# Sharing a third channel group of a depthwise convolution between three engines, and taking the key transposes out of the sample group's fixed order, in a hybrid decoder layer

## The chip, the cores and the metric

The kernel runs on one core of one Trainium2 chip. The metric is the time of one launch of the program on the device, in microseconds (us), and less is better. In the text PE is TensorE, DVE is VectorE, ACT is ScalarE, POOL is GpSimd and SP is the engine that issues most transfers.

## The reference

One layer of a decoder is computed for 512 prompt tokens and for 64 sample tokens (8 sequences of 8). Cut to what the change touches:

```python
a_glu, b_glu, q, k, v, qi, ki, wi, g_c, g_a = jnp.split(h @ w_in, IN_SPLITS, axis=-1)
glu = a_glu * jax.nn.sigmoid(b_glu)
buf = jnp.concatenate([conv_prefix, glu], axis=1)
# 31 taps per channel, 512 channels = 4 groups of 128 partitions
c = silu(layer_norm(causal_depthwise_conv(buf, conv_w, conv_b), lnc_g, lnc_b))
conv_branch = c @ w_conv_out
# sample tokens: indexer scores over 4096 cached keys, the best 256, then attention over them
idx, valid = select_keys(indexer_scores(qi, wi, ki_all), q_pos, topk)
kg = jnp.where(sel, cache_k[layer, phys, off], gather_rows(k_new, nidx))
vg = jnp.where(sel, cache_v[layer, phys, off], gather_rows(v_new, nidx))
o = attend_selected(q, kg, vg, valid)
mix = (sigmoid(g_c) * conv_branch + sigmoid(g_a) * (o @ w_attn_out)) @ w_o
```

After that come a layer norm, a mixture of 32 experts, a gated side branch and a second layer norm, which the change leaves alone. Everything is float32.

## The kernel before, in words

All work of the layer stands in one list of jobs, `JOBS`. Every engine walks through the same list and does its share of each job; semaphores count what is ready. The list has these stages.

**First stage (to about 86 us).** Keys of the indexer are fetched and turned, and the scores of the 64 sample tokens are made.

**Second stage (to about 346 us).** DVE picks the best 256 keys, eight at a time, in 32 rounds (L1962 to L1964). While it does, PE runs the input projections and ten gate jobs, each job one PSUM bank of four that take turns (`RING = 4`): a job may start only when ACT has emptied the bank of the job four places earlier. ACT empties every job and, right after some of them, makes "products" for the convolution: one tap times the gated input, 816 columns (`conv_product`, L1629; the first of a channel group is L1622). Which product stands after which job is written out in `PRODUCTS`, worked out from the jobs' costs. POOL adds the products up (`conv`, L1048), with three product buffers between the two engines: ACT may be three products ahead and then waits. Two channel groups of the four (`PCONV = 2`) are done in this way. The gated input of a channel group is POOL's too (`gated`, L1014 to L1018), and it needs that group's `aS` job. Between the adds stand four pieces of the page lookup (`physical_rows`, L1027 to L1034): each turns the page numbers of one chunk of the selected keys into cache rows, and waits until DVE has finished the chunk. `MAP_AT` says before which add the second and third stand. When the fourth is done, DVE merges the two lists of each token, PE turns the list (`offs`, L1295), ACT writes the offsets, and POOL can begin to gather.

**Third stage (about 346 to 745 us).** The 64 sample tokens are worked in 16 groups of four. For each group POOL issues eight gathers of keys and eight of values (L1069, two per token and kind). For groups 0 to 7 the keys are turned on PE (`T`, L1179, four jobs per group, each two banks of four transposes) and copied by ACT (L1645). For groups 8 to 15 DVE makes the logits itself (`KQ`, L2037 and L2042). Then come the logits (`QK`: L1191 and L1209), a maximum on DVE (L2167), the exponentials on ACT (L1651), the turned weights (`PT`, L1218 and L1219), the values (`PV`, L1227 and L1230), a mask on DVE (L2179) and a sum over groups (`OS`, L1237). There is one set of buffers for keys and one for values: POOL gathers the keys of group g+1 once the logits of group g are done, and the values of group g+1 once the values of group g have been used. POOL's order is keys, values, keys, values.

Beside it run the prompt's attention (`pi`, `qk`, `pt`, `pv` on PE; rounds, `unit` and `weigh` on DVE), the rest of the convolution branch (`cv`, `cn`, `cbP`, `cbS`) and the gates (`gaP`, `gaS`). The other two channel groups of the convolution, 62 taps, are DVE's there (`conv_tap`, L2052 and L2054, two instructions per tap); `cv` cannot start before they are done.

The order of this third stage comes from `merged`: it takes the next job from one of three streams (sample, prompt, branch) as the letters of `PICKS` say, and lays out DVE's work by its own costs, with taps and rounds as filling. In the sample stream the order within a group is fixed: QK, EX, PT, the first two T of the next group, PV, the last two T, OS.

**The rest (745 to 1268 us).** Output projections, layer norm, router, experts, second layer norm.

## Time and profile before

| | |
|---|---|
| runs of the kernel before, us | 1278.06, 1266.98, 1277.57 |
| median | 1277.57 |
| the profiled execution | 1269.41, its span 1267.6 |
| PE busy | 1138.5 (90%) |
| DVE busy | 744.5 (59%) |
| ACT busy | 432.1 (34%) |
| POOL busy | 537.0 (42%) |
| PE busy in the third stage (345 to 745 us) | 336.1 of 400 |
| gathers of keys and values | 256 issues, 264.4 us busy |

The span is the time from the first to the last instruction of one execution; the rest of the launch lies around it. Shares of busy time are averages over stages with different limits, so the rows that count are those of one stage: which engine has no gaps there, and what the last of the engines waits for. In the second stage DVE has none, in the third stage several engines take turns.

### The profile page before, as it was taken

How to read it: one execution, taken by the hardware profiler on the slowest of the kernel's cores; microseconds unless marked ns; L12 is line 12 of the kernel's file. 1: busy time of each engine (PE TensorE's matmuls, PEld its weight loads, DVE VectorE, ACT ScalarE, POOL GpSimd, SP SyncE). 2: the span in 40 equal slices, each digit the busy share in tenths (PEclk: the TensorE clock that was granted, in tenths of full speed). 3: DMA queues.
4: the chain of work that ended last, by engine and by line, in shares of the span. 5: the costliest groups of instructions: out<-in, count | busy, mean ns of one | idle time of the engine just before them, and what ended most of it. 6: DMA issues, size and time to landing. Idle time of an engine off the chain costs nothing.

```text
span 1267.6 us, 22339 instructions
## 1 busy us (share of the span) xinstructions
PE 1138.5 (90%) x8697; PEld 725.2 (57%) x8697; DVE 744.5 (59%) x1368; ACT 432.1 (34%) x952; POOL 537.0 (42%) x488
## 2 busy tenths in 40 slices
PE   4899999989989767668999999999999999999896
PEld 4525677778654333324556645888885555555442
DVE  1459999999998888787764513444533221111116
ACT  4540124364354366666322212123112222222220
POOL 5000067887876765576677700000003433433310
PEclk9899999989999887778999999999899999998998
DMA  9511222223166565586799853024278999999935
GB/s 323 214 47 42 85 75 70 67 75 104 50 198 172 169 200 166 150 252 202 226 315 299 284 179 105 17 73 161 84 275 323 403 418 411 369 419 415 417 116 194
DMA packets 86200, 258.61 MB, mean 204 GB/s; under 512 B 13311, under 2 KB 45939, under 8 KB 77191
## 3 DMA queue, kind: packets, MB, share of 16 engines
q1 hardware_dynamic: 54816, 168.79, 35.7%
q0 software_dynamic: 28720, 84.98, 21.1%
q10 hardware_dynamic: 2559, 3.40, 0.8%
q8 instruction: 70, 1.15, 0.4%
q14 instruction: 35, 0.29, 0.1%
HBM read 356.78 MB, written 19.05 MB: 296 GB/s over the span
## 4 chain that ended last, share of the span: by engine, by line
PE 45%; DVE 29%; DMA 13%; POOL 7%; issue 4%; ACT 1%; SPq 1%; DVEq 0%; POOLq 0%; ACTq 0%
DMA arena<-in_w_ex 9%; POOL arena L1069 7%; PE ps L1522 7%; DVE arena L1963 6%; DVE arena L1962 6%; DVE arena L1964 6%; PE ps L1139 6%; PE ps L1145 5%; PE ps L1369 4%; PE ps L1544 3%; PE ps L1361 3%; DMA arena<-in_w_in 2%; PE ps L1532 2%; DMA arena<-in_cache_kv,arena 2%; PE ps L1227 2%
## 5 line engine op out<-in xcount | busy, mean ns | idle before, releaser
L1069 POOL DMA_INDIRECT arena<-in_cache_kv,arena x256 | 264.4, 1033 | 118.5 <-issue 73.7
L1139 PE MATMUL ps<-arena 128*128 128x288 f32 (+2 forms) x1120 | 294.4, 424 | 1.1 <-ACT arena L1688 1.1
L1139 PEld LDWEIGHTS ps<-arena 128*128 128x128 f32 (+1 forms) x1120 | 209.6, 189 | 83.3 <-issue 30.3
L1522 PE MATMUL ps<-arena 128*32 128x256 f32 x2144 | 145.4, 388 | 17.1 <-DMA arena<-in_w_ex 16.1
L1095 POOL DMA_INDIRECT scr_ypair<-arena x67 | 66.9, 999 | 165.7 <-ACT arena L1896 161.2
L2359 DVE TENSOR_TENSOR arena<-arena,ps 128x64 f32<-128x64 f32 x67 | 14.9, 222 | 183.3 <-ACT arena L1890 183.3
L1611 ACT ACTIVATE arena<-ps 128x256 f32<-128x256 f32 (+5 forms) x138 | 57.6, 428 | 183.1 <-PE ps L1361 57.2
L1048 POOL TENSOR_TENSOR arena<-arena 128x816 f32<-128x816 f32 x58 | 103.0, 1775 | 17.4 <-ACT arena L1629 10.6
L1145 PE MATMUL ps<-arena 128*128 128x256 f32 (+4 forms) x544 | 105.3, 357 | 0.8 <-ACT arena L1833 0.6
L1145 PEld LDWEIGHTS ps<-arena 128*128 128x128 f32 (+1 forms) x544 | 92.4, 194 | 13.3 <-issue 1.8
L1522 PEld LDWEIGHTS ps<-arena 128*32 128x32 f32 x2144 | 66.3, 111 | 56.8 <-issue 21.9
L1089 POOL DMA_INDIRECT arena<-scr_x,arena x34 | 35.4, 1040 | 145.9 <-DVE arena L2338 135.3
L1962 DVE MAX8 arena<-arena 128x8 f32<-128x2052 f32 x32 | 73.6, 2299 | 1.1
L1544 PE MATMUL ps<-arena 128*32 128x256 f32 x1072 | 72.6, 388 | 1.0 <-issue 0.9
L1963 DVE FIND_INDEX8 arena<-arena 128x8 uint32<-128x2052 f32 x32 | 73.3, 2290 | 0.0
L1964 DVE MATCH_REPLACE8 arena<-arena 128x2052 f32<-128x2052 f32 x32 | 73.0, 2280 | 0.0
L1179 PE MATMUL ps<-arena 128*128 128x128 f32 x256 | 42.5, 320 | 33.6 <-DMA arena<-in_cache_kv,arena 25.7
L1629 ACT ACTIVATE arena<-arena 128x816 f32<-128x816 f32 x60 | 57.0, 970 | 28.6 <-POOL arena L1048 26.3
L1361 PE MATMUL ps<-arena 128*128 128x288 f32 (+1 forms) x192 | 64.1, 483 | 0.0
L1179 PEld LDWEIGHTS ps<-arena 128*128 128x128 f32 x256 | 34.1, 165 | 47.6 <-DMA arena<-in_cache_kv,arena 31.8
L2054 DVE SCALAR_TENSOR_TENSOR arena<-arena 128x512 f32<-128x512 f32 x120 | 56.9, 516 | 2.0
L2037 DVE TENSOR_TENSOR arena<-arena 128x1024 f32<-128x1024 f32 x32 | 39.2, 1224 | 30.4 <-DMA arena<-in_cache_kv,arena 29.4
(342 smaller groups left out, 1649.2 us busy)
## 6 DMA issues: line engine op xcount, KB each, us to landing
arena<-in_w_ex SPq DMA_DIRECT2D x67, 2048.0 KB
arena<-in_w_ex SPq DMA_DIRECT2D x67, 1024.0 KB
arena<-in_w_in SPq DMA_DIRECT2D x20, 1024.0 KB, 5.6
arena<-scr_q SPq DMA_DIRECT2D x32, 256.0 KB, 5.0
arena<-in_cache_kv,arena POOLq DMA_INDIRECT x256, 3.9
arena<-in_w_o SPq DMA_DIRECT2D x4, 1024.0 KB, 5.3
arena<-in_w_pg SPq DMA_DIRECT2D x4, 1024.0 KB, 6.1
arena<-scr_ypair SPq DMA_DIRECT2D x4, 1024.0 KB, 7.9
```

The lines of the kernel that those rows point to most:

```text
L1048: nc.gpsimd.tensor_tensor(a[:, 0:CLEN], a[:, 0:CLEN], p[:, 0:CLEN], ALU.add).then_inc(conv_add, 1)
L1069: pl.indirect_dma_start(unit_rows[:, 2 * j + t, half * H * HD:(half + 1) * H * HD], None, I["cache_kv"].rearrange("n (h d) -> (n h) d", h= ...
L1095: pl.indirect_dma_start(S["ypair"].rearrange("n (h d) -> (n h) d", h=4), bass.IndirectOffsetOnAxis(ap=slist[:, q:q + 1], axis=0), ys[q % Y ...
L1139: mm = nc.tensor.matmul(out, w[:, k], hT[:, k, a:b], start=(k == 0), stop=(k == KC - 1))
L1145: mm = nc.tensor.matmul(out, hT[:, k, at:at + rows], w[:, k], start=(k == 0), stop=(k == KC - 1))
L1179: mm = nc.tensor.transpose(PS[4 + m % 2][:, c * P:(c + 1) * P], unit_rows[:, 2 * j + t, c * P:(c + 1) * P], ident)
L1361: mm = nc.tensor.matmul(ps[:, 0:n], w[:, c], src[:, c, at:at + n], start=(c == 0), stop=(c == CC - 1))
L1522: mm = nc.tensor.matmul(PS[2 + q % 2][r:r + BLK, 0:F], xT[:, p % 3, j, 64 * h + BLK * sub:64 * h + BLK * sub + BLK], w[:, 4 * h + j, half, ...
L1544: mm = nc.tensor.matmul(PS[5 + q % 2][BLK * quarter:BLK * quarter + BLK, 0:D // 4], hidT[:, q % 2, c, :], w[:, c, quarter * (D // 4):(quar ...
L1962: step(V.max(m, work))
L1963: V.max_index(idxu[:, r * 8:r * 8 + 8], m, work)
L1964: step(V.match_replace(work, m, work, TAKEN))
```

## The change

Of the third channel group 12 taps are taken from DVE. ACT makes twelve more products for them, and POOL adds them up (11 adds) and writes the partial sum to where DVE then goes on from tap 12. So POOL makes 71 adds in place of 60 and DVE 50 taps in place of 62. The projection jobs are ordered so that each `aS` job comes after its own `bP`, `bS`, `aP` (b and a alternate for each channel group of 128), the products start after the fifth of these jobs and not after the ninth, and the pieces of POOL's other work get new places: the first page lookup before add 8, the second before add 34, the third before add 60, and the gated inputs of the second and third channel groups before adds 20 and 48. `AWAY` holds three stretches of the products' calendar in which none is planned.

The jobs that turn keys (or multiply them) become a stream of their own, `key_jobs`, with a letter `k` in `PICKS`; only two rules bind it: no key job of group g before the logits of group g-1, and no logits before the four key jobs of their group. The planner's time from a gather's issue to its landing goes to 3.5, and `PICKS` is new.

The diff, with the old letters of `PICKS` cut:

```diff
+SHARED = 12
+TAPS = [CW] * PCONV + [SHARED, 0]
+ADDS = sum(n - 1 for n in TAPS if n)
...
 def sample_jobs():
-    def keys(g):
-        return [("KQ" if g >= BY_VECTOR else "T", g, j) for j in range(GQ)] if g < NGR else []
-    jobs = keys(0)
     for g in range(NGR):
-        turned = keys(g + 1)
-        jobs += [("QK", g), ("EX", g), ("PT", g)] + turned[:2] + [("PV", g)] + turned[2:] + [("OS", g)]
+        jobs += [("QK", g), ("EX", g), ("PT", g), ("PV", g), ("OS", g)]
     return jobs
+def key_jobs():
+    return [("KQ" if g >= BY_VECTOR else "T", g, j) for g in range(NGR) for j in range(GQ)]
...
-    waiting = [("conv", c, w) for c in range(PCONV, CC) for w in range(CW)]
+    waiting = [("conv", c, w) for c in range(PCONV, CC) for w in range(TAPS[c], CW)]
...
-            landed[("T", g, j) if keys else ("PV", g)] = pool + (2.3 if keys else 2.8)
+            landed[("T", g, j) if keys else ("PV", g)] = pool + LANDING
...
+        if job[0] in ("T", "KQ") and job[1]:
+            return ("QK", job[1] - 1) not in pe_end
+        if job[0] == "QK":
+            return ("KQ" if job[1] >= BY_VECTOR else "T", job[1], GQ - 1) not in jobs
...
-HOP, GATHER, TABLE = 0.12, 2.62, 1.28
+HOP, GATHER, LANDING, TABLE = 0.12, 2.62, 3.5, 1.28
+PICKS = ("pbpbpkkkpkppppspsbspppskppkpkksspspbsppppskkpkpkpsssbbskskkkpsppspspsbppskpkkpkbsppspspbsbksbkkkbpss"
...
     for g in range(2):
-        for kind in "ba":
-            for c in range(2):
+        for c in range(2):
+            for kind in "ba":
                 jobs += [(kind + "P", g, c), (kind + "S", g, c)]
...
-MAP_AT = {1: 21, 2: 46}
+MAP_AT = {0: 8, 1: 34, 2: 60}
+GATED_AT = {1: 20, 2: 48}
+AWAY = ((16.0, 27.0), (79.0, 90.0), (143.0, 152.0))
-_beside = RINGED[NUM[("bP", 1, 0)]:NUM[GATES[3][0]]]
-_pace = sum(cost(_j) for _j in _beside) / (PCONV * CW + 0.5)
+_beside = RINGED[NUM[("bP", 0, 1)]:NUM[GATES[3][0]]]
+def beside_pool(t):
+    return t - sum(min(max(t - a, 0.0), b - a) for a, b in AWAY)
+_pace = beside_pool(sum(cost(_j) for _j in _beside)) / (sum(TAPS) + 0.5)
 for _j in _beside:
-    _due += cost(_j) / _pace
-    _take = min(int(_due), PCONV * CW - _n)
-    PRODUCTS[_j] = range(_n, _n + _take)
+    _at += cost(_j)
+    _upto = min(int(beside_pool(_at) / _pace), sum(TAPS))
+    PRODUCTS[_j] = range(_n, _upto)
...
             def conv(c):
-                for w in range(1, CW):
+                for w in range(1, TAPS[c]):
                     for i, at in MAP_AT.items():
                         if k == at:
                             physical_rows(i)
+                    for i, at in GATED_AT.items():
+                        if k == at:
+                            gated(i)
...
-            for c in range(PCONV):
-                gated(c)
-            physical_rows(0)
-            for c in range(PCONV):
+            gated(0)
+            for c in range(PCONV + 1):
                 conv(c)
             physical_rows(3)
-            for c in range(PCONV, CC):
-                gated(c)
+            gated(PCONV + 1)
...
             def conv_tap(c, w):
-                if w == 0:
+                if w == TAPS[c]:
                     dve.wait_ge(glu_ready, 1 + 3 * c + 3)
+                if w and w == TAPS[c]:
+                    dve.wait_ge(conv_ready, c + 1)
+                    dve.wait_ge(conv_add, ADDS)
```

**Three places in the order of instructions.** First ACT, at the first products. The program names are few, since nearly all tiles lie in one tensor, `arena`, and the PSUM banks are `ps`; so the lines and shapes tell the instructions apart. Before, from the emptying of the ninth projection job (L1730) on; L1622 and L1629 are products, the others empty a job:

```order
L1730 ACTIVATE arena<-ps 128x288
L1622 ACTIVATE arena<-arena 128x816
L1739 ACTIVATE arena<-ps 128x288
L1629 ACTIVATE arena<-arena 128x816 x2
L1730 ACTIVATE arena<-ps 128x288
L1629 ACTIVATE arena<-arena 128x816
L1739 ACTIVATE arena<-ps 128x288
L1629 ACTIVATE arena<-arena 128x816 x2
```

In the change, from the emptying of the seventh to the twelfth job (the emptyings are L1745, L1753 with L1754, L1747 and L1756; L1646 is a product):

```order
L1745 ACTIVATE arena<-ps 128x288
L1646 ACTIVATE arena<-arena 128x816 x2
L1753 ACTIVATE arena<-ps 128x224
L1754 ACTIVATE arena<-ps 128x8x8
L1646 ACTIVATE arena<-arena 128x816 x2
L1747 ACTIVATE arena<-ps 128x288
L1756 ACTIVATE arena<-ps 128x288
L1745 ACTIVATE arena<-ps 128x288
L1753 ACTIVATE arena<-ps 128x224
L1754 ACTIVATE arena<-ps 128x8x8
L1646 ACTIVATE arena<-arena 128x816 x2
```

Products 4 to 7 stand after the seventh and eighth job, then come three jobs with none, and products 8 and 9 stand after the twelfth. Before, the first product came only after the ninth.

Second POOL, from its first gated input. Before (L1014 to L1018 a gated input, L1027 to L1034 the page lookup, L1048 an add):

```order
L1014 TENSOR_TENSOR arena<-arena 128x64
L1016 TENSOR_TENSOR arena<-arena 128x512
L1018 COPY arena<-arena 128x8x8
L1014 TENSOR_TENSOR arena<-arena 128x64
L1016 TENSOR_TENSOR arena<-arena 128x512
L1018 COPY arena<-arena 128x8x8
L1027 TENSOR_TENSOR arena<-arena 128x2560
L1031 TENSOR_TENSOR arena<-arena 128x1280
L1031 TENSOR_TENSOR arena<-arena 128x640
L1031 TENSOR_TENSOR arena<-arena 128x320
L1031 TENSOR_TENSOR arena<-arena 128x160
L1034 TENSOR_TENSOR arena<-arena 128x80
L1048 TENSOR_TENSOR arena<-arena 128x816 x21
```

In the change (L1031 to L1035 a gated input, L1044 to L1051 the page lookup, L1068 an add):

```order
L1031 TENSOR_TENSOR arena<-arena 128x64
L1033 TENSOR_TENSOR arena<-arena 128x512
L1035 COPY arena<-arena 128x8x8
L1068 TENSOR_TENSOR arena<-arena 128x816 x8
L1044 TENSOR_TENSOR arena<-arena 128x2560
L1048 TENSOR_TENSOR arena<-arena 128x1280
L1048 TENSOR_TENSOR arena<-arena 128x640
L1048 TENSOR_TENSOR arena<-arena 128x320
L1048 TENSOR_TENSOR arena<-arena 128x160
L1051 TENSOR_TENSOR arena<-arena 128x80
L1068 TENSOR_TENSOR arena<-arena 128x816 x12
```

The second gated input has gone from here to before add 20, and eight adds now stand ahead of the page lookup. The eighth of them needs product 8.

Third PE, sample group 2 from its turned weights to its sum over groups. Before (L1218 and L1219 PT, L1179 T of the next group, L1227 and L1230 PV, L1237 OS):

```order
L1218 MATMUL ps<-arena 128x128 x2
L1219 MATMUL ps<-arena 64x128
L1179 MATMUL ps<-arena 128x128 x16
L1227 MATMUL ps<-arena 8x512 x8
L1230 MATMUL ps<-arena 8x512 x4
L1179 MATMUL ps<-arena 128x128 x16
L1237 MATMUL ps<-arena 64x512
```

In the change (L1235 and L1236 PT, L1196 T, L1244 and L1247 PV, L1316 a score of the prompt, L1254 OS):

```order
L1235 MATMUL ps<-arena 128x128 x2
L1236 MATMUL ps<-arena 64x128
L1196 MATMUL ps<-arena 128x128 x8
L1244 MATMUL ps<-arena 8x512 x8
L1247 MATMUL ps<-arena 8x512 x4
L1196 MATMUL ps<-arena 128x128 x24
L1316 MATMUL ps<-arena 128x512
L1254 MATMUL ps<-arena 64x512
```

Of the four key jobs of the next group, two stood ahead of the values, and now one does; three stand behind.

## Rows read from the trace of the kernel before

**Rows 1.** Timeline of PE: start, length, line, wait in brackets; four starts of logits.

```profile
365.60 0.73 PE L1191 MATMUL ps<-arena 128*8 128x320 f32 x8
...
436.52 0.72 PE L1191 MATMUL ps<-arena 128*8 128x320 f32 x8
...
570.18 1.16 PE L1191 MATMUL ps<-arena 128*8 128x320 f32 x8
...
727.09 0.73 PE L1191 MATMUL ps<-arena 128*8 128x320 f32 x8
```

**Rows 2.** Busy time by window: window, length, PE, PEld, DVE, ACT, POOL, clock, DMA.

```profile
437.00:463.00 26.00, 19.69 (x143) 11.81 (x139) 22.45 (x77) 13.58 (x31) 17.14 (x18) 0.87 0.64 190
463.00:488.00 25.00, 18.18 (x133) 9.55 (x129) 21.41 (x73) 17.55 (x44) 15.25 (x17) 0.80 0.58 167
488.00:510.50 22.50, 15.19 (x127) 8.50 (x119) 21.15 (x61) 15.93 (x35) 15.33 (x17) 0.85 0.65 187
510.50:541.00 30.50, 20.65 (x153) 10.75 (x149) 24.04 (x68) 19.30 (x46) 16.87 (x19) 0.78 0.54 153
541.00:571.00 30.00, 19.55 (x131) 7.41 (x123) 23.46 (x61) 17.79 (x45) 22.41 (x22) 0.77 0.82 257
...
683.00:706.00 23.00, 23.00 (x173) 14.80 (x169) 11.38 (x14) 7.17 (x12) 17.20 (x18) 1.00 0.90 296
```

**Rows 3.** Instruction groups of GpSimd, 345 to 430 and 436 to 556 us.

```profile
L1069 POOL DMA_INDIRECT arena<-in_cache_kv,arena x56 | 62.5, 1116 | 22.9 <-issue 16.1 <-PE ps L1230 4.5 <-ACT arena L1772 2.2
...
L1069 POOL DMA_INDIRECT arena<-in_cache_kv,arena x79 | 76.8, 972 | 44.2 <-issue 22.5 <-PE ps L1230 21.7
```

**Rows 4.** Timeline of GpSimd at the fifth sample group.

```profile
453.57 0.95 POOL L1069 DMA_INDIRECT arena<-in_cache_kv,arena  x1 [0.30 <-issue]
458.50 0.94 POOL L1069 DMA_INDIRECT arena<-in_cache_kv,arena  x1 [3.98 <-PE ps L1230]
```

**Rows 5.** Timeline of PE, fourth and fifth sample groups.

```profile
424.90 1.97 PE L1179 MATMUL ps<-arena 128*128 128x128 f32 x8 [7.44 <-DMA arena<-in_cache_kv,arena]
...
455.32 1.90 PE L1227 MATMUL ps<-arena 128*8 128x512 f32 x16
```

**Rows 6.** Instruction groups of VectorE by shape, 340 to 785 us.

```profile
L2054 DVE SCALAR_TENSOR_TENSOR arena<-arena 128x512 f32<-128x512 f32 x60 | 45.1, 752 | 2.0
...
L2054 DVE SCALAR_TENSOR_TENSOR arena<-arena 128x64 f32<-128x64 f32 x60 | 16.8, 280 | 0.0
...
L2078 DVE MAX8 arena<-arena 128x8 f32<-128x256 f32 x16 | 6.8, 425 | 0.4
```

**Rows 7.** Timeline of GpSimd, 170 to 341 us.

```profile
170.69 0.31 POOL L1014 TENSOR_TENSOR arena<-arena 128x64 f32<-128x64 f32 x1 [6.03 <-ACT arena L1737]
...
172.49 4.46 POOL L1027 TENSOR_TENSOR arena<-arena 128x2560 f32<-128x2560 f32 x1
...
183.53 15.49 POOL L1048 TENSOR_TENSOR arena<-arena 128x816 f32<-128x816 f32 x8
...
299.35 3.61 POOL L1027 TENSOR_TENSOR arena<-arena 128x2048 f32<-128x2048 f32 x1 [2.46 <-DVE arena L1974]
...
308.44 24.37 POOL L1048 TENSOR_TENSOR arena<-arena 128x816 f32<-128x816 f32 x13
...
340.80 0.32 POOL L1034 TENSOR_TENSOR arena<-arena 128x32 f32<-128x32 f32 x1
```

**Rows 8.** Timeline of ScalarE, 158 to 186 us, then its products, 139 to 345 us.

```profile
158.50 0.41 ACT L1728 ACTIVATE arena<-ps 128x288 f32<-128x288 f32 x1 [3.47 <-PE ps L1139]
...
185.66 0.41 ACT L1739 ACTIVATE arena<-ps 128x288 f32<-128x288 f32 x1 [2.61 <-PE ps L1139]
...
L1629 ACT ACTIVATE arena<-arena 128x816 f32<-128x816 f32 x60 | 57.0, 970 | 28.6 <-POOL arena L1048 26.3 <-POOL arena L1051 2.1
```

**Rows 9.** Timelines of VectorE and PE, where the lists end.

```profile
341.95 1.20 DVE L1989 SCALAR_TENSOR_TENSOR arena<-arena 128x256 f32<-128x256 f32 x1
...
345.92 0.44 PE L1295 MATMUL ps<-arena 64*128 64x64 f32 x2 [2.90 <-DVE arena L1993]
```

More of the change, by code:

```diff
@@ L163, in sample_jobs @@
 def sample_jobs():
-    def keys(g):
-        return [("KQ" if g >= BY_VECTOR else "T", g, j) for j in range(GQ)] if g < NGR else []
-    jobs = keys(0)
+    jobs = []
     for g in range(NGR):
-        turned = keys(g + 1)
-        jobs += [("QK", g), ("EX", g), ("PT", g)] + turned[:2] + [("PV", g)] + turned[2:] + [("OS", g)]
-    return jobs
+        jobs += [("QK", g), ("EX", g), ("PT", g), ("PV", g), ("OS", g)]
+    return jobs
+def key_jobs():
+    return [("KQ" if g >= BY_VECTOR else "T", g, j) for g in range(NGR) for j in range(GQ)]
 def columns(kind):
@@ L191, in merged @@
 def merged(picks):
-    streams = {"sample": sample_jobs(), "prompt": prompt_jobs(), "branch": branch_jobs()}
+    streams = {"sample": sample_jobs(), "prompt": prompt_jobs(), "branch": branch_jobs(), "keys": key_jobs()}
     jobs, vector_order, ring, slots = [], [], [], []
@@ L360, in merged @@
     return dve, jobs, vector_order + waiting
-HOP, GATHER, TABLE = 0.12, 2.62, 1.28
-PICKS = ("pbpbpssppssppsspppbpppsppsppsppsspsbssspbspsssssppsssppsssssssssbsbppssbpssspsppsbpsbsppsbpsssbppssp"
-         "ssbpsbbsssppssbsspspspbppsssssppbppspsppspssspbsbppspppspppssppsppsspppppsspssbsppsppbpspppssbpsppsp"
-         "bppsbspbsssbsbssssbbsbsbbssbsbssssbsbsbssbsbsssbsssbssbpsssbsbssbsssbsssbssbsbsssbsbsbs")
-STREAM = {"s": "sample", "p": "prompt", "b": "branch"}
+HOP, GATHER, LANDING, TABLE = 0.12, 2.62, 3.5, 1.28
+PICKS = ("pbpbpkkkpkppppspsbspppskppkpkksspspbsppppskkpkpkpsssbbskskkkpsppspspsbppskpkkpkbsppspspbsbksbkkkbpss"
+         "spppsbkpskkbksppsppbspsppbkbpskkksppsppspbsppkppksppkkbbpspsppppspkkppskbspppbkpspppsppkpsppbkspspps"
+         "pkbpkpbbsskpbkkbsbspkbbsbsksbkbsbksbbkbsssbkskkbsbskbsksbksbsbkkbsskskbsbksbkbsssbsbsbs")
+STREAM = {"s": "sample", "p": "prompt", "b": "branch", "k": "keys"}
 ATTENTION, VJOBS = merged([STREAM[k] for k in PICKS])[1:]
@@ L482 @@
 CHUNKS = [(0, 80), (80, 160), (160, 224), (224, TOPS)]
-MAP_AT = {1: 21, 2: 46}
+MAP_AT = {0: 8, 1: 34, 2: 60}
+GATED_AT = {1: 20, 2: 48}
+AWAY = ((16.0, 27.0), (79.0, 90.0), (143.0, 152.0))
 CLEN = PRE + NP + NB * (PRE + NQ) - PRE
 PRODUCTS = {}
-_beside = RINGED[NUM[("bP", 1, 0)]:NUM[GATES[3][0]]]
-_pace = sum(cost(_j) for _j in _beside) / (PCONV * CW + 0.5)
-_n, _due = 0, 0.0
-for _j in _beside:
-    _due += cost(_j) / _pace
-    _take = min(int(_due), PCONV * CW - _n)
-    PRODUCTS[_j] = range(_n, _n + _take)
-    _n += _take
-    _due -= _take
-assert _n == PCONV * CW
+_beside = RINGED[NUM[("bP", 0, 1)]:NUM[GATES[3][0]]]
+def beside_pool(t):
+    return t - sum(min(max(t - a, 0.0), b - a) for a, b in AWAY)
+_pace = beside_pool(sum(cost(_j) for _j in _beside)) / (sum(TAPS) + 0.5)
+_n, _at = 0, 0.0
+for _j in _beside:
+    _at += cost(_j)
+    _upto = min(int(beside_pool(_at) / _pace), sum(TAPS))
+    PRODUCTS[_j] = range(_n, _upto)
+    _n = _upto
+assert _n == sum(TAPS)
 GROUP_AT = {g[2]: n for n, g in enumerate(WGROUPS)}
@@ L1046, in conv @@
                         pl.wait_ge(conv_add, k)
-                    if w < CW - 1:
+                    if w < TAPS[c] - 1:
                         nc.gpsimd.tensor_tensor(a[:, 0:CLEN], a[:, 0:CLEN], p[:, 0:CLEN], ALU.add).then_inc(conv_add, 1)
@@ L1053, in conv @@
                         nc.gpsimd.tensor_tensor(convo[:, c, 0:NP], a[:, 0:NP], p[:, 0:NP], ALU.add).then_inc(conv_add, 1)
[L1054 to L1057 removed]
+            gated(0)
+            for c in range(PCONV + 1):
                 conv(c)
             physical_rows(3)
[L1060 to L1063 removed]
+            gated(PCONV + 1)
+            pl.wait_ge(conv_ready, PCONV + 1)
+            pl.wait_ge(conv_add, ADDS)
             pl.wait_ge(drained, after("offs"))
@@ L1325, in _ @@
                     if a[0] == 0:
-                        pe.wait_ge(conv_ready, PCONV)
-                        pe.wait_ge(conv_add, PCONV * (CW - 1))
-                        pe.wait_ge(conv_dve, 2 * CW * (CC - PCONV))
+                        pe.wait_ge(conv_ready, PCONV + 1)
+                        pe.wait_ge(conv_add, ADDS)
+                        pe.wait_ge(conv_dve, 2 * (CW * (CC - PCONV) - SHARED))
                     for c in range(CC):
@@ L2055, in conv_tap @@
                     ins.then_inc(conv_dve, 1)
-                dve.wait_ge(conv_dve, 2 * ((c - PCONV) * CW + w) + 2)
+                dve.wait_ge(conv_dve, 2 * ((c - PCONV) * CW + w - SHARED) + 2)
             def head_score(t, h):
@@ L2060, in head_score @@
                 if (t, h) == (1, 0):
-                    dve.wait_ge(conv_ready, PCONV)
-                    dve.wait_ge(conv_add, PCONV * (CW - 1))
+                    dve.wait_ge(conv_ready, PCONV + 1)
+                    dve.wait_ge(conv_add, ADDS)
                 wi = kw[:, t, 64 + h:65 + h]
```

2 lines of the change are left out of this document (removed).

## The prediction

> **What bounds the kernel now.** I read three views, in this order. The table of busy time by window says which engine has no gaps. From 87 to about 345 us that is DVE with its rounds of top-k; PE and POOL only have to be ready when the lists are. From 345 to 745 us it changes. In the five sample groups from 437 to 571 us [rows 2] no engine is full: DVE is busy 112.5 of 134 us, PE 93.3, and TensorE's granted clock is 0.77 to 0.87. From 683 to 706 us PE is busy all 23.0. The timeline of PE then gives the cadence: from the logits of group 0 to those of group 3 it takes 70.9 us, to those of group 8 another 133.7, to those of group 15 another 156.9 [rows 1]. The waits say who sets it. POOL waits 21.7 us between 436 and 556 us for PE to have used the values, and 4.5 before 430 us [rows 3]. The timelines show how: the last key gather of group 4 starts at 453.57, and then POOL stands 3.98 us [rows 4], because the values of group 3 (PE at 455.32 [rows 5]) come in PE's order behind two key jobs of group 4, and those wait for keys that were issued only a few us before. It is a loop: keys late, values late, the next values' gathers late.
>
> Two things decide, then: when the lists are ready, and the cadence of groups 3 to 7. The part after 745 us hangs on the end of this stage and moves with it.
>
> **Part 1: twelve taps to ACT and POOL, second stage.** DVE saves 12 taps of 0.75 + 0.28 us [rows 6], 12.4 us, in the third stage. ACT makes 12 products more beside idle time. The question is whether POOL is still at its fourth page lookup when DVE has the last chunk, at about 335.5 us. I follow POOL. Jobs of PE come every (185.66 - 158.50) / 7 = 3.88 us [rows 8]. The gated input of the first channel group can start two jobs sooner. But product 8, which the eighth add needs, stands behind the twelfth job, which ACT empties at 185.66 [rows 8]; the first page lookup stands behind that add in POOL's order. With the two parts of the emptying and a product of 0.97 us [rows 8], add 8 can start at 187.2. The seven adds before it are done by about 175, so POOL stands idle for some 12 us, in the stretch that `AWAY` keeps free of products. From there it has no gap: add 8 until 189.1; lookups of 11.0 (172.49 to 183.53), 11.0 and 9.1 us (299.35 to 308.44), two gated inputs of 1.8 (170.69 to 172.49), and 63 adds, each 24.37 / 13 = 1.87 to 15.49 / 8 = 1.94 us [rows 7], less 1.2 us since the last add of each group is shorter. That ends at 189.1 + 31.1 + 3.6 + 116.6 to 121.0 = 340.4 to 344.8. The fourth lookup took 5.6 us (335.5 to 341.1 [rows 7]) and would now end at 346.0 to 350.4, not 341.1. DVE came to the place that needs it only at 341.95 [rows 9], 0.85 us later. So the lists, and with them all gathers, are 4.0 to 8.4 us late; I take 6.5. PE waited 2.90 us for the lists [rows 9]. It will itself be held up, since ACT, with three product buffers, waits for POOL before it empties banks. Four banks cover 3 x 3.88 = 11.6 us of that, less beside the short jobs that turn the prompt's keys; about 10 us of PE's idle fit under 2.9 + 6.5 + what the chain from list to offsets takes. I cost it at nothing, and this cover is the thinnest in the sum. The gated input of one channel group, 1.8 us, is no longer behind the fourth lookup, but it lay beside DVE's merging.
>
> **Part 2: the key stream, third stage.** In groups 0 to 2 PE has the same key, value and logit jobs as before; one gate job of about 4 us comes into these groups, and PE's wait of 7.44 us for keys [rows 5] goes. PE is then full. I take 1 us longer, bounds 3 shorter and 5 longer. In groups 3 to 7 the values now stand ahead of the key jobs or behind one of them, so that POOL's wait shrinks from about 4 us per group to about 1. What comes next as a limit? POOL's own issuing: 80 gathers x (0.972 + 0.30) us [rows 3] = 101.8. PE: 93.3 busy, less at a higher clock. DVE: 112.5 before; four taps (4.1), five of the smallest rounds (two instructions of about 0.43 each, 4.3 [rows 6]) and two prompt units leave this stretch, one large round comes, so about 104.5. DVE is the next limit, and it cannot be filled wholly: once per group it waits for the values, which wait for their gathers. I add 8.5 us of such waits, where 21.5 were before, and take 113, against 133.7: 20.7 saved. Bounds: 106 (27.7 saved), if the waits almost vanish, and 126 (8 saved), if DVE's place in the order makes the exponentials late as often as before. In groups 8 to 15 PE is full already; I take 1.5 us saved, bounds 5 saved and 2 lost. The twelve taps bring nothing on top: they are what lets DVE follow the new cadence.
>
> Of TensorE's clock: the five windows miss 0.13 to 0.23 of full speed, together 25 us of their 134 [rows 2], and the transposes that came after the wait of 7.44 us took 1.97 us [rows 5]. I count none of it, as DVE and POOL limit the new cadence. The Trainium skill, in TensorE: Matmul & The Clock Gate (HAM oscillation), says that an engine which waits for data again and again is put back to half its clock each time, and that the cost is half of the throttled time. By that rule PE itself would get up to 25 us back in these windows once it no longer waits, 4 us more than I count for them, and the sum would go to 1255 in place of 1259 (with the 4 us explained below). The trace agrees on the clock; whether that time is on the path it doesn't show.
>
> **The sum**, against the profiled execution of 1269.4 us (span 1267.6): + 6.5 + 1 - 20.7 - 1.5 = -14.7, so 1254.7. The median of the runs, 1277.6, is 8.2 above the profiled execution, since two of the three runs lie near 1278 and one at 1267. Nothing tells me where the median of the changed kernel falls between the two, and I take half of the difference: **1259 us**. All times below have the same 4 us in them.
>
> **The cases.**
>
> 1. As above: lists 4 to 8 us late, cadence 16 to 26 us better. 1259, by its bounds 1250 to 1270. For it: both steps can be counted out in rows. Chance 0.50.
> 2. POOL catches up, and the lists are not late: the idle 12 us are made up somewhere I do not see. 1259 - 6.5 = 1252. Against it: POOL's sum of work from 189 us has no gap left. Chance 0.10.
> 3. The cadence hardly moves, because DVE or ACT takes POOL's place: only 6 us are saved of the 21, the lists are late. 1259 + 15 = 1274. For it: DVE is busy 84% in these groups already [rows 2], and its order puts rounds ahead of maxima. Chance 0.24.
> 4. Slower. ACT stands at products that wait for POOL during the three lookups and the 12 us gap, PE's four banks run out, and the gate jobs end long after the lists. PE could lose as much as 11.0 + 11.0 + 9.1 us of lookups, 31 us, against an end of PE's work at 345.92 - 2.90 = 343.0 us [rows 9]; offsets would be made at 374 in place of 346, gathers 28 us late. With the cadence's 21 us that gives 1259 + 21.5 = 1280; it decides from the point at which PE stands for more than about 11 us before the lists. Against it: before, ACT's waits for POOL never stopped PE but for a few us. Chance 0.08.
> 5. More than forecast: with fewer waits PE is at its full clock, exponentials and copies come sooner, and groups 3 to 7 come near POOL's 102 us. 1259 - 11 = 1248. Chance 0.08.
>
> One that does nothing is not among them: the order of the instructions shows both moves.
>
> **Range and chances.** The range is 1243 to 1277: it takes in cases 1, 2, 3 and 5, with 4 us to either side for where the median falls. About 1% is what a measurement of this kernel can tell from no change. Against the median of 1277.6 the bound for faster is 1264.8: 0.40 of case 1, nearly all of 2 and 5, some 0.54 together. Slower by over 1%, above 1290, needs case 4 with a cadence like case 3's: 0.06. The rest, 0.40, is no change.
>
> **What would show it.** In the profile of the changed kernel: POOL idle from about 175 to 187 us, waiting for ACT; the first lookup from about 189 to 200; POOL's last add of the third channel group at 340 to 345; the first gather of keys at 352 to 356 in place of 347.7; PE waiting in the second stage for ACT, in all near 10 us; then logits of group 3 to logits of group 8 in 113 us (106 to 126), POOL's waits for PE at L1086 in all below 20 us, granted clock above 0.85, DVE busy over 90% in those groups; and the end of the third stage at 730 us. The forecast is wrong if the first gather does not move, if the cadence stays above 25 us a group, or if PE stands for more than 11 us before the lists.

## The result and the profile after

The changed kernel takes 1266.2 us (median of 20 runs, 1257.0 to 1271.2). The kernel before takes 1276.7 in the same comparison. The ratio is 0.991, with an interval of 0.990 to 0.993: 11 us faster. I had forecast 1259 us, 18.6 below the shown median. The direction and the range held; the gain was a little more than half of the forecast one. By the bound that I had set for faster, 1264.8 us, the result falls to what I had called no change (0.40), though the interval leaves out 1. One of the 20 runs of the kernel before took 1915.9 us; without it its median is 1276.6. The profiled execution took 1268.0 us, its span is 1266.3.

**First a common mark.** Two profiled executions differ before the change begins. The row of the first top-k instruction shows it (count; shortest, median, longest ns; start of the first and last). First the kernel before:

```profile
L1962 DVE MAX8 arena<-arena x32: 2299/2299/2301, 87.4 to 324.0; 128x8 f32<-128x2052 f32 x32
```

and the changed kernel:

```profile
L1979 DVE MAX8 arena<-arena x32: 2298/2299/2300, 92.8 to 328.7; 128x8 f32<-128x2052 f32 x32
```

The first stage has the same instructions in both and ended 5.4 us later here. So I count from the first MAX8, and end at the logits of group 15. That stretch was 727.1 - 87.4 = 639.7 us before and is 720.85 - 92.8 = 628.1 now: 11.6 us shorter, and the medians say 11.

**The cadence.** The timeline of PE of the changed kernel at logits 0, 3, 8 and 15, answering to [rows 1]:

```profile
384.91 1.25 PE L1208 MATMUL ps<-arena 128*8 128x320 f32 x8
...
451.60 0.72 PE L1208 MATMUL ps<-arena 128*8 128x320 f32 x8
...
561.86 1.26 PE L1208 MATMUL ps<-arena 128*8 128x320 f32 x8
...
720.85 0.73 PE L1208 MATMUL ps<-arena 128*8 128x320 f32 x8
```

The three pieces are 66.7, 110.3 and 159.0 us, where 70.9, 133.7 and 156.9 stood. The windows of the changed kernel (columns as in [rows 2]), groups 0 to 2, 3 to 7 and 8 to 14:

```profile
385.00:452.00 67.00, 62.64 (x415) 33.16 (x418) 58.77 (x130) 34.95 (x64) 51.11 (x48) 0.99 0.68 193
452.00:562.00 110.00, 84.99 (x631) 40.90 (x623) 100.10 (x304) 76.69 (x189) 78.60 (x81) 0.85 0.70 206
562.00:721.00 159.00, 149.51 (x1121) 91.21 (x1117) 104.05 (x180) 59.38 (x130) 116.58 (x114) 0.98 0.83 269
```

In groups 3 to 7 DVE is now busy 100.1 of 110 us, 91%. POOL's waits in the third stage (line waited at, who is waited for, sum, times, longest), first the one for the values in the kernel before, then those of the changed kernel:

```profile
POOL arena L1069 <- PE ps L1230: 42.5, 13, 8.4
...
POOL arena L1086 <- PE ps L1247: 17.4, 10, 4.8
POOL arena L1086 <- ACT arena L1789: 2.9, 1, 2.9
POOL arena L1086 <- PE ps L1226: 2.2, 2, 1.9
```

POOL stood 42.5 us for the values, and now it stands 17.4.

**The lists.** POOL's timeline of the changed kernel around the first and the fourth page lookup:

```profile
176.98 3.97 POOL L1068 TENSOR_TENSOR arena<-arena 128x816 f32<-128x816 f32 x2 [0.24 <-ACT arena L1646]
192.50 1.63 POOL L1068 TENSOR_TENSOR arena<-arena 128x816 f32<-128x816 f32 x1 [11.55 <-ACT arena L1646]
194.09 4.46 POOL L1044 TENSOR_TENSOR arena<-arena 128x2560 f32<-128x2560 f32 x1
...
331.36 20.67 POOL L1068 TENSOR_TENSOR arena<-arena 128x816 f32<-128x816 f32 x10
...
353.67 1.90 POOL L1044 TENSOR_TENSOR arena<-arena 128x1024 f32<-128x1024 f32 x1
355.65 3.00 POOL L1048 TENSOR_TENSOR arena<-arena 128x512 f32<-128x512 f32 x4
358.73 0.25 POOL L1051 TENSOR_TENSOR arena<-arena 128x32 f32<-128x32 f32 x1
...
363.91 2.91 POOL L1086 DMA_INDIRECT arena<-in_cache_kv,arena  x1 [2.95 <-ACT arena L1789]
```

POOL stands 11.55 us for a product at the eighth add, and only then starts the first lookup. At the fourth lookup it comes late. DVE and then PE wait for that (timelines of DVE and of PE):

```profile
359.10 0.44 DVE L2006 SCALAR_TENSOR_TENSOR arena<-arena 128x256 f32<-128x256 f32 x1 [6.34 <-POOL arena L1051]
```

```profile
362.31 0.31 PE L1312 MATMUL ps<-arena 64*128 64x64 f32 x2 [2.27 <-DVE arena L2010]
```

From the first MAX8 to the first gather it is 271.1 us; before it was 347.66 - 87.4 = 260.3. The lists cost 10.8 us, and the cadence gives back more.

### The profile page after: what moved, and what is told of

It is laid out like the page before. It is cut to its first block, busy times and chain, and to the rows that moved or that the text cites. A ratio compares the mean times of both kernels' runs of the same rounds, so it can differ in the third digit from the quotient of the medians.

```text
span 1266.3 us, 22346 instructions
## 1 busy us (share of the span) xinstructions
PE 1145.6 (90%) x8697; PEld 727.3 (57%) x8697; DVE 737.5 (58%) x1344; ACT 442.3 (35%) x963; POOL 561.8 (44%) x500
## 3 DMA queue, kind: packets, MB, share of 16 engines
q0 software_dynamic: 28720, 84.98, 21.2%
## 4 chain that ended last, share of the span: by engine, by line
PE 51%; POOL 20%; DMA 14%; DVE 8%; issue 4%; ACT 2%; SPq 1%; POOLq 0%; DVEq 0%; ACTq 0%
PE ps L1156 11%; POOL arena L1068 9%; DMA arena<-in_w_ex 9%; POOL arena L1086 8%; PE ps L1539 7%; PE ps L1162 6%; PE ps L1386 4%; PE ps L1378 4%; PE ps L1561 3%; DMA arena<-in_w_in 2%; PE ps L1549 2%; DMA arena<-in_cache_kv,arena 2%; PE ps L1244 2%; POOL arena L1048 2%; PE ps L1410 1%
## 5 line engine op out<-in xcount | busy, mean ns | idle before, releaser
L1539 PE MATMUL ps<-arena 128*32 128x256 f32 x2144 | 148.2, 395 | 15.1 <-DMA arena<-in_w_ex 14.1
L1068 POOL TENSOR_TENSOR arena<-arena 128x816 f32<-128x816 f32 x68 | 127.1, 1870 | 25.1 <-ACT arena L1646 16.9
L1646 ACT ACTIVATE arena<-arena 128x816 f32<-128x816 f32 x71 | 68.0, 973 | 59.3 <-POOL arena L1068 55.0
L1561 PE MATMUL ps<-arena 128*32 128x256 f32 x1072 | 73.3, 391 | 1.0 <-issue 0.9
L1378 PE MATMUL ps<-arena 128*128 128x288 f32 (+1 forms) x192 | 66.7, 499 | 3.3 <-DVE arena L2169 3.3
L2054 DVE TENSOR_TENSOR arena<-arena 128x1024 f32<-128x1024 f32 x32 | 39.1, 1221 | 34.0 <-issue 23.1
L1386 PE MATMUL ps<-arena 128*128 128x256 f32 x256 | 55.9, 380 | 0.8 <-DVE arena L2138 0.8
L1196 PE MATMUL ps<-arena 128*128 128x128 f32 x256 | 38.5, 297 | 16.3 <-DMA arena<-in_cache_kv,arena 9.9
L1386 PEld LDWEIGHTS ps<-arena 128*128 128x128 f32 x256 | 48.5, 190 | 7.3 <-issue 0.9
```

Of the source, the lines that this page charges most:

```text
L1068: nc.gpsimd.tensor_tensor(a[:, 0:CLEN], a[:, 0:CLEN], p[:, 0:CLEN], ALU.add).then_inc(conv_add, 1)
L1378: mm = nc.tensor.matmul(ps[:, 0:n], w[:, c], src[:, c, at:at + n], start=(c == 0), stop=(c == CC - 1))
L1386: mm = nc.tensor.matmul(ps[0:rows, 0:GW], mixT[:, k, at:at + rows], w[:, k], start=(k == 0), stop=(k == KC - 1))
L1539: mm = nc.tensor.matmul(PS[2 + q % 2][r:r + BLK, 0:F], xT[:, p % 3, j, 64 * h + BLK * sub:64 * h + BLK * sub + BLK], w[:, 4 * h + j, half, ...
L1561: mm = nc.tensor.matmul(PS[5 + q % 2][BLK * quarter:BLK * quarter + BLK, 0:D // 4], hidT[:, q % 2, c, :], w[:, c, quarter * (D // 4):(quar ...
L1646: nc.scalar.activation(prod[:, k % 3, 0:CLEN], glu[:, c, w:w + CLEN], cp, scale=tap).then_inc(prod_ready, 1)
```

## The experiments

Two columns of the table come from each kernel's trace: first MAX8 to first gather, and first MAX8 to logits 15, with the three pieces between logits. The ratio is the recorded one, to the kernel before measured beside it on one chip; the quotient of the two medians can lie a few thousandths from it (0.979 for e11).

```
kernel                       gather  0-3    3-8    8-15   MAX8 to L15  ratio (interval)
before                       260.3   70.9   133.7  156.9  639.7        1
changed                      271.1   66.7   110.3  159.0  628.1        0.991 (0.990-0.993)
e1 lookup one add earlier    260.9   68.2   110.1  159.2  616.9        0.983 (0.979-0.987)
e2 taps alone                272.0   71.3   129.9  154.5  646.3        1.005 (1.002-1.007)
e3 keys alone                260.4   66.7   120.2  167.2  634.8        0.995 (0.992-0.998)
e4 e3, 12 taps left out      260.8   66.3   111.4  159.4  618.7        0.986 (0.982-0.989)
e5 e3, order for 62 taps     260.3   71.3   121.0  155.1  625.7        0.990 (0.986-0.993)
e6 e1, keys tied, replanned  261.0   77.3   130.3  146.2  631.5        0.995 (0.992-0.998)
e7 e1, order planned again   260.9   67.3   109.7  161.4  620.6        0.981 (0.977-0.985)
e8 before, six more adds     273.1   70.2   133.9  159.0  653.5        one run
e9 e1, 12 more left out      260.9   67.6   108.3  156.5  613.4        0.972 (0.968-0.976)
e10 changed, again           271.1   69.7   112.3  155.2  628.2        0.991 (0.988-0.994)
e11 e1, again                261.1   67.5   110.2  161.2  620.1        0.982 (0.977-0.986)
```

**Is the 11.5 us gap the lateness of the lists?** One number moves the first lookup ahead of the eighth add:

```diff
-MAP_AT = {0: 8, 1: 34, 2: 60}
+MAP_AT = {0: 7, 1: 34, 2: 60}
```

> The changed kernel, with its first page lookup one add earlier in POOL's order (behind the seventh add in place of the eighth). Theory A: the first gather of the changed kernel is late because POOL stands 11.55 us at the eighth add and later has no gap. Then the lookup fills that time, POOL's last add of the third group ends some 11 us earlier (near 343 us of a span whose first stage ends at 92 us), the first gather comes 8 to 11 us earlier, and the median is 1257 us, 0.984 of the kernel before (0.981 to 0.987). Rival B: it is late because ACT stands at products while POOL looks up pages, and PE's banks run out. Then the lookup's new place moves only the stall: first gather at most 3 us earlier, 1264 us, 0.990.

POOL's timeline of this kernel, at the same two places:

```profile
168.93 3.98 POOL L1068 TENSOR_TENSOR arena<-arena 128x816 f32<-128x816 f32 x2 [0.25 <-ACT arena L1646]
172.86 4.47 POOL L1044 TENSOR_TENSOR arena<-arena 128x2560 f32<-128x2560 f32 x1
...
334.27 1.90 POOL L1044 TENSOR_TENSOR arena<-arena 128x1024 f32<-128x1024 f32 x1
336.24 3.28 POOL L1048 TENSOR_TENSOR arena<-arena 128x512 f32<-128x512 f32 x4
339.60 0.32 POOL L1051 TENSOR_TENSOR arena<-arena 128x32 f32<-128x32 f32 x1
...
345.68 2.77 POOL L1086 DMA_INDIRECT arena<-in_cache_kv,arena  x1 [3.47 <-ACT arena L1789]
```

The lookup fills the time in which POOL stood, and the wait before the eighth add is gone. The first MAX8 starts at 84.8 here, so the gather comes 260.9 us behind it, 0.6 later than in the kernel before. Theory A holds, with all of the 10 us. This version is faster than both kernels. It was run again, and the changed kernel beside it:

> The changed kernel again, beside the one with the earlier lookup on one chip: 0.991 of the kernel before (0.989 to 0.993), in theory A and B alike; its first gather some 10 us later, from the first top-k instruction on, than that of the kernel with the earlier lookup.

> The changed kernel with the first page lookup behind the seventh add, once more. Theory A (POOL's idle wait of 11.5 us was the whole lateness of the lists): 0.983 of the kernel before, 8 to 12 us faster than the changed kernel on the same chip. Rival B (the first comparison caught a favourable chip): within 4 us of the changed kernel.

They gave 0.991 and 0.982 on one chip (medians 1261.4 and 1248.3), and 271.1 against 261.1 us to the first gather. The lookup's place is worth 8 us (stretches of e10 and e11) to 13 us (their medians). ACT, which stood 53.4 us for POOL's adds in the changed kernel (130 to 345 us), stands 22.6 in e1: rival B's stall did not move, it shrank.

**The taps alone.** The second stage is the changed one; key jobs, `blocked`, landing times and `PICKS` are those of before:

```diff
-        jobs += [("QK", g), ("EX", g), ("PT", g), ("PV", g), ("OS", g)]
+        turned = keys(g + 1)
+        jobs += [("QK", g), ("EX", g), ("PT", g)] + turned[:2] + [("PV", g)] + turned[2:] + [("OS", g)]
...
```

> The changed second stage alone: twelve taps on ACT and POOL, products begun sooner, lookups where the change puts them; the order of the third stage and its key jobs as in the kernel before, planned with the 50 taps that are left to DVE. Theory A (the two parts are separate, the cadence comes from the key stream): first gather 11 us late, logits of group 3 to logits of group 8 in 130 to 135 us, median 1286 us, 1.007 of the kernel before (1.004 to 1.010). Rival B (DVE's freed 12.4 us carry the cadence): group 3 to group 8 in 125 us or less, and the time is that of the kernel before or lower, at most 1.001.

The lists are 11.7 us late. Groups 3 to 7 take 129.9 us, 3.8 less than before, and groups 8 to 14 2.4 less. In sum 6.6 us slower, 1.005. The ratio is theory A's and the piece lies at the edge of A's: without the key stream the 12.4 us that DVE saves bring about 6 (two pieces of one execution; by the medians, 7 us slower, about 4 to 5).

**The keys alone.** The second stage is that of before, DVE has all 62 taps, and the third stage has the key stream with the `PICKS` of the change. Against the changed kernel, cut to the third stage:

```diff
-    waiting = [("conv", c, w) for c in range(PCONV, CC) for w in range(TAPS[c], CW)]
+    waiting = [("conv", c, w) for c in range(PCONV, CC) for w in range(CW)]
...
```

> The key stream alone: the third stage planned as in the change, all 62 taps on DVE, the second stage exactly as in the kernel before. Theory A: lists on time (first gather about 16 us before that of the changed kernel, 11 us without the difference of the first stage), and DVE has room for the twelve taps: logits of group 3 to logits of group 8 in 110 to 116 us, median 1254 us, 0.982 of the kernel before (0.979 to 0.985), faster than the full change. Rival B (the taps are what lets DVE follow): group 3 to group 8 in 120 to 126 us, median 1266 us or more, 0.991 or above.

Rival B came out. The window of groups 3 to 7 and the wait of PE for the taps in it:

```profile
442.00:562.00 120.00, 84.29 (x628) 40.26 (x627) 107.28 (x322) 76.94 (x188) 81.02 (x82) 0.83 0.66 193
```

```profile
PE ps L1336 <- DVE arena L2060: 8.6, 1, 8.6
```

DVE is busy 107.3 us, 7.2 more than in the changed kernel, and the groups take 9.9 us longer. L2060 is the tap: PE stands 8.6 us until the last one is done.

**The keys alone, twelve taps left out.**

```diff
-    waiting = [("conv", c, w) for c in range(PCONV, CC) for w in range(CW)]
+    waiting = [("conv", c, w) for c in range(PCONV, CC) for w in range(12 if c == PCONV else 0, CW)]
...
-                if w == 0:
+                first = 12 if c == PCONV else 0
+                if w == first:
```

> As the key stream alone, and DVE leaves out the first twelve taps of the third channel group (the sums lack them), the order planned for the 50 that are left. It gives what the twelve taps are worth on DVE at no price on ACT and POOL. Theory A: 0 to 4 us faster than the key stream alone, 1252 us, 0.980 to 0.982 of the kernel before. Rival B: the 12.4 us are on the path through the third stage, and it is 9 to 13 us faster than the key stream alone.

It gives 0.986 where e3 gave 0.995: 12.5 us by the ratios, 11.5 in the medians and 16.1 in the stretch, for 12.4 us less of DVE. That is rival B again. And it is no faster than e1, where ACT and POOL do the taps (618.7 against 616.9 and 620.1): once the lookup stands right, ACT and POOL do them for nothing.

**Was e3's order unfair to 62 taps?** The same kernel with picks searched for 62 taps, by the time that the kernel's own planner gives an order:

```diff
-PICKS = ("pbpbpkkkpkppppspsbspppskppkpkksspspbsppppskk...
+PICKS = ("bbkkkpkpspppppsbpsksk...
```

> The key stream alone again (all 62 taps on DVE, the second stage as in the kernel before), with an order of the third stage that was planned for 62 taps; in the run before this one the order was the change's, planned for 50, and PE stood 8.6 us at the transposes of the conv branch until a tap was done. Theory A (DVE's room is what counts, wherever the taps stand): 0.993 to 0.998 of the kernel before, group 3 to group 8 in 118 us or more. Rival B (the order was wrong for 62 taps, DVE has the room): group 3 to group 8 in 115 us or less, no wait of over 4 us for a tap, 0.985 to 0.989.

0.990, between the theories. Groups 3 to 7 still take 121.0 us, as A says; the wait of PE for a tap is down from 8.6 to 2.2 us, as B says. The planned order puts a part of the load elsewhere, so the whole is 9.1 us shorter than e3. Against e1 and e11, with 50 taps on DVE, it is 6 to 9 us longer. So of e3's 16 us about half was its order, and half is DVE's room.

**Is it the stream, or only the new plan?** As e1, but two key jobs before and two behind the values of each group as in the kernel before, with the landing of 3.5 us and `PICKS` planned for that:

```diff
-        jobs += [("QK", g), ("EX", g), ("PT", g), ("PV", g), ("OS", g)]
+        turned = keys(g + 1)
+        jobs += [("QK", g), ("EX", g), ("PT", g)] + turned[:2] + [("PV", g)] + turned[2:] + [("OS", g)]
...
-PICKS = ("pbpbpkkkpkppppspsbspppskppkpkksspspbsppppskk...
+PICKS = ("ppppbssspppspssbbsssss...
```

> No key stream: two key jobs before and two behind the values of each group, as in the kernel before; all else as in the changed kernel with the earlier lookup (twelve taps on ACT and POOL, landing of 3.5 us in the planner), and the order of the third stage planned anew. Theory A (the freedom of the key jobs is what breaks the loop of keys and values): lists on time, group 3 to group 8 in 124 us or more, POOL's waits for the values above 15 us, 0.993 to 0.998 of the kernel before. Rival B (planning anew for the real landing and 50 taps is what counts, not the stream): group 3 to group 8 in 116 us or less, 0.987 or below.

POOL's wait for the values between 440 and 570 us:

```profile
POOL arena L1080 <- PE ps L1241: 28.7, 6, 8.8
```

Theory A: the loop of keys and values is still there, 130.3 us in groups 3 to 7, and the whole is 0.995 with the lists on time. The stream is worth 11 to 15 us on top of the taps. Against the kernel before, e6 is 8.2 us shorter in the stretch and 6 by the ratio: that is what the taps and the new plan bring without the stream, once the lists are on time.

**More of the same.** The stream planned once more, with the values ahead of all four key jobs in groups 2 to 6:

```diff
-PICKS = ("pbpbpkkkpkppppspsbspppskppkpkksspspbsppppskk...
+PICKS = ("ppppppbkbpkkkppppssbs...
```

> The changed kernel with the earlier lookup, and its third stage planned once more by the same planner, with more key jobs behind the values of the same group. Theory A (from logits to logits DVE's work sets the pace and any good order gives it): within 3 us of the earlier lookup alone, 0.981 to 0.985. Rival B (the values' place before the key jobs is what counts, and more of it gives more): 5 us or more faster, 0.979 or below.

109.7 us in groups 3 to 7 and 0.981: as e1 within what can be measured. Theory A.

**And fewer taps still.** e1, and DVE starts the third channel group at tap 24:

```diff
-    waiting = [("conv", c, w) for c in range(PCONV, CC) for w in range(TAPS[c], CW)]
+    waiting = [("conv", c, w) for c in range(PCONV, CC) for w in range(TAPS[c] + 12 * (c == PCONV), CW)]
...
```

> The changed kernel with the earlier lookup, and DVE leaves out twelve further taps (38 are left of 62; the sums lack taps 12 to 23 of the third channel group). Theory A (in groups 3 to 7 DVE's room still sets the pace, tap by tap): another 6 to 12 us, group 3 to group 8 in 100 to 104 us or groups 0 to 2 shorter, 0.973 to 0.978 of the kernel before. Rival B (with 50 taps another limit has taken over: POOL's issuing of gathers, or PE in groups 0 to 2 and 8 to 15): at most 4 us faster than the earlier lookup alone, 0.980 or above, group 3 to group 8 in 107 us or more.

The trace and the medians differ here. In the stretch, 12.4 us less of DVE give 3.5 to 6.7 us, and only 1.8 of them in groups 3 to 7, which is rival B. The ratio of 0.972 is theory A's, and the median is 10 us lower than that of e11. Most of that lies behind logits 15: 531.9 us to the end of the span, against 543.7 in e11. That part varies by itself (545.4 in the changed kernel, 536.5 in its repetition e10). The outcome of the convolution, from which the later stages go on, is another here, but so it is in e4, where this part took 545.0; why it was short stays open. For the pace of groups 3 to 7 I read their piece alone. Its window, and what POOL stood idle in it with no other engine to wait for:

```profile
443.73:552.00 108.27, 82.54 (x628) 39.95 (x628) 87.33 (x260) 76.77 (x188) 78.42 (x82) 0.88 0.72 212
```

```profile
POOL arena L1086 <- issue: 24.4, 78, 0.9
```

DVE is busy only 81% here. POOL's 78.4 us busy and the 24.4 between its gathers make 102.8 of 108.3, and waits for PE are most of the rest (3.9 and 1.9). In the changed kernel the same three are 78.9, 23.5 and 8.2 of 110.3. So with 50 taps on DVE, POOL's own issuing already stands next to DVE, and with 38 it stands alone; that it is what holds the piece there is read from these sums, and no run made the issuing shorter.

**Do POOL and DVE hold each other up?** In the changed kernel single adds are longer than any of before. The timeline of DVE, and that of POOL over the same time:

```profile
240.34 2.83 DVE L1991 TENSOR_TENSOR arena<-arena 128x2560 f32<-128x2560 f32 x1
```

```profile
240.39 4.26 POOL L1068 TENSOR_TENSOR arena<-arena 128x816 f32<-128x816 f32 x1
```

The longest add before was 1.94 us. To see the tie by itself, the kernel before got six more adds behind its fourth lookup, where DVE merges the lists:

```diff
             physical_rows(3)
+            for i in range(6):
+                pl.wait_ge(conv_add, PCONV * (CW - 1) + i)
+                nc.gpsimd.tensor_tensor(acc[:, 1, 0:CLEN], acc[:, 0, 0:CLEN], prod[:, 0, 0:CLEN], ALU.add).then_inc(conv_add, 1)
```

> The kernel before, with six more adds of 128x816 on POOL behind the fourth page lookup, on buffers that nothing reads any more. Theory A (a small DVE operation waits until the instruction that POOL is in has ended): DVE's operations of 0.42 us in the merge of the lists beside the adds take 1.5 to 2.0 us each, the lists are ready 6 to 9 us later, while DVE's top-k instructions of 2.3 us elsewhere keep their time. Rival B (no such tie; the slow ones in the changed kernel had another cause): they stay at 0.42 us and the lists come on time. In both the gathers are late by the 11 us of the adds, and the whole is about 10 us slower.

POOL's row, and DVE's beside and behind it:

```profile
346.89 12.42 POOL L1062 TENSOR_TENSOR arena<-arena 128x816 f32<-128x816 f32 x6
```

```profile
346.84 0.42 DVE L1989 TENSOR_TENSOR arena<-arena 64x256 f32<-64x256 f32 x1
347.29 2.04 DVE L1990 TENSOR_TENSOR arena<-arena 64x256 f32<-64x256 f32 x1
349.36 2.03 DVE L1992 SCALAR_TENSOR_TENSOR arena<-arena 128x256 f32<-128x256 f32 x1
351.43 1.90 DVE L1993 COPY arena<-arena 64x256 f32<-64x256 f32 x1
353.36 2.09 DVE L1994 TENSOR_TENSOR arena<-arena 64x256 f32<-64x256 f32 x1
...
361.30 0.42 DVE L1999 TENSOR_TENSOR arena<-arena 64x256 f32<-64x256 f32 x1
```

One DVE operation goes through per add: 12.42 / 6 = 2.07 us, and DVE's take 1.9 to 2.1 each, where the same ones took 0.29 to 0.44 when not held. PE takes the lists at 359.73, 8.7 us later than before by the first MAX8, and the first gather is 12.8 us later. Theory A. The Trainium skill, in SBUF — State Buffer (Who interferes with whom), says that a DVE instruction with two SBUF inputs contends with a GpSimd instruction that reads SBUF, and that the port pair which the two share is an exclusive lock. These rows agree, both ways round. By the page, DVE instructions with one input and outside its two-port modes are spared. MAX8 agrees: 2.30 us with adds beside it and without. The copy at 351.43 has one input and was held. The page says that copies can enter a two-port mode and then contend; no run here shows the mode.

## Why the prediction was half right

- **The lists.** I took 6.5 us, bounds 4.0 to 8.4. It is 10.8, twice. It was mis-sized by 4.3 us, in both executions alike; groups 0 to 2 were off by more, 5.2 us, in one of them. Less the 5.4 us of the first stage, the eighth add starts at 187.1 (forecast 187.2), so the place of the gap was right to a tenth (11.55 us long, forecast some 12). But I priced the adds at 1.87 to 1.94 us from rows in which they ran almost all beside one-input top-k instructions. From 192.50 to 353.71 POOL has 64 adds in 126.7 us (161.2 less three lookups and two gated inputs, 34.5): 1.98 each. The surplus over my price is the lock of e8. By the timelines of POOL and DVE, 46 of these adds ran beside top-k instructions alone and took 1.89 us each from start to start, as priced. The 15 that met other DVE instructions, those of the page tables and the first of the merge, took 2.36: 7.0 us more in all (the last add of each channel group, three, is split and not counted). Three of them were held longest, at 240.39, 303.74 and 339.31 us, for 4.26, 3.72 and 2.64 us. Before, POOL stood and waited for the table at these points. The fourth lookup thus ended at 353.6 on the old clock, not at 346.0 to 350.4. The remedy, one number, stood in my own paragraph: the lookup was behind the very add that waited.
- **PE in the second stage.** I expected about 10 us of waits for ACT that cost nothing. Four rows of PE's waits from 130 to 366 us in the changed kernel:

```profile
PE ps L1503 <- ACT arena L1758: 3.9, 2, 2.7
PE ps L1503 <- ACT arena L1764: 2.9, 1, 2.9
PE ps L1503 <- ACT arena L1749: 2.9, 1, 2.9
PE ps L1156 <- ACT arena L1749: 2.3, 1, 2.3
```

  They are 12.0 us (all of PE's waits for ACT there 13.2, before 4.0), and PE still waited 2.27 for the lists at 362.31. The cover held, barely. Case 4, slower by PE's banks, did not come.
- **From the first gather to logits 0** I had no term. It is 21.0 us in place of 17.9. PE is busy 17.8 us of it in place of 15.0, with 80 and 79 matmuls: the granted clock is 0.83 there and was 0.96. In the new order eight scores of the prompt stand between the last key transposes and the logits, 2.08 us, where four stood, 0.70. The other kernels with the stream show 18.0 to 21.2, e6 without it 16.7.
- **Groups 0 to 2** I took as 1 us longer. They are 4.2 shorter, and 1.2 in the repetition e10. By my own terms, a gate job of 4 us in and a wait of 7.44 us [rows 5] out, it should have been 3.4 shorter; the 1 us had no working behind it. PE's idle time in the piece fell from 11.7 to 4.4 us, in both. What differs is its clock: granted 0.99 in the changed kernel and 0.94 in e10 (before 0.93), with PE busy 62.3 and 65.4 us (before 59.2). So the 7.4 us less idle time hold in both, and the clock makes the difference of 3 us between two executions of one kernel. For groups 3 to 7 it is 0.85 (0.81 before), and I had asked for more than 0.85; the 1255 us that the clock might have brought did not come.
- **Groups 3 to 7** I put at 113 us, and 110.3 is measured (again 112.3). The mechanism is right in its parts: POOL's wait for values shrank to below 20 us, DVE is over 90% busy, and e6 shows that without the stream the loop stays. Two things were missing. DVE is not alone as the next limit: POOL's issuing, forecast at 101.8 us and 78.9 + 23.5 = 102.4 measured, is as near (e9). And a part of the saving is work that moved on: the period from logits 8 to logits 9 is longer in every kernel with the stream, 23.1 to 34.0 us, than in those without, 18.1 to 21.6.
- **The twelve taps** I called without a gain of their own, and at the same time what lets DVE follow. The second half is right: with the stream, they are worth 6 to 9 us against an order planned for 62 taps, and 12 to 16 against the same order. e2 shows about 6 us without the stream, so the first half was too low: the taps bring about as much without the stream as with it. That they let DVE follow shows in groups 3 to 7: 11 us with the stream (121.0 and 110.1), 4 without (133.7 and 129.9).
- **Groups 8 to 15** I took as 1.5 us shorter; they are 2.1 longer: 5.8 in the one period between logits 8 and 9, from 21.6 to 27.4 us, less 3.7 in the rest. More work stands in that period: DVE is busy 23.8 us in it and PE 22.0, where it was 19.1 and 17.1. In e10 the piece is 155.2, so its sign I can't tell from chance.
- **The end of the third stage** I put at 730 us, 15 before the mark of 745. But 745 was only a round mark: the last matmul of the stage stood at 751.4 before. It is at 745.2 now, 739.8 by the common mark, in line with the 11.6 us.

The sum of the pieces: + 10.8 + 3.1 - 4.2 - 23.4 + 2.1 = -11.6, where I had -14.7 and added 4 us for the median. That the sum held this well is in part luck: the lists (10.8), groups 0 to 2 and groups 8 to 15 lay outside my bounds for them, and the piece up to logits 0 had no term. The errors were + 4.3, + 3.1 and + 3.6 on one side and - 5.2 and - 2.7 on the other. The profiled execution, forecast at 1254.7, took 1268.0: 3.1 us are these errors, 5.4 the first stage, 4.9 the part behind logits 15 (545.4 in place of 540.5). The shown median of before, 1277.6, was of three runs; over 20 it was 1276.7, and the changed kernel's was 1266.2, 1.9 us below its profiled execution, where before it lay 7.3 above. Of the 4 us that I added, for half of that difference, no run shows anything.

What stays open: why the stream's groups 8 to 15 and the part behind them vary by several us in the same kernels (155.2 and 159.0 us for the piece in the changed one), and why the granted clock of groups 0 to 2 does.

## What to carry to other kernels

When an engine's order has a planned idle stretch, put there the work that needs nothing from the others, and check which instruction stands directly ahead of it: here a lookup of 11 us stood one add too late, and that one place cost as much as the whole change gained. Before parts of a change are judged alone, give each what it needs: the taps alone brought a loss, but it was the late lookup's. With the lookup in its place and a plan of its own, the version without the stream (e6) brought 6 to 8 us, the keys alone 5 to 6 (13 to 14 with an order of their own), both together 19 to 24, about the sum of the two. An order that was planned for one load is no fair test of another: plan it anew before the load is blamed.

## What the runs showed of the hardware

- POOL and DVE held each other up for whole instructions, in both directions: DVE's 0.42 us operations took 1.9 to 2.1 us beside adds of 2.07, and an add took 4.26 us beside a DVE operation of 2.83 us. An add of 816 columns took 1.89 us from start to start beside top-k instructions and 2.36 beside others (46 and 15 adds). A price read from a row holds only beside the same neighbour.
- The first stage, the same instructions in all kernels, ended anywhere between 84.8 and 95.1 us (first MAX8), and the part behind logits 15 took 536.5 and 545.4 us in two executions of one kernel. The same kernel ran groups 0 to 2 at a granted clock of 0.99 and of 0.94, in 66.7 and 69.7 us. A comparison by a mark inside the program agreed with the ratios within 5 us for all kernels but e9 (9 us); with the medians e11 is off too (8 us).
